# Layer 0: norms, up-projections and rotation in one stage, with split f32r products of 384 columns

## The reference, cut to what matters

```python
p = h @ w_in                                  # 1024 -> 384 + 256 + 32 + 512 + 128 + 128
cq, ckv, kr, gq, gk, gv = split(p)
qa  = rmsnorm(cq, q_norm) @ w_q_up            # 384 -> 8 heads x (64 + 32)
kva = rmsnorm(ckv, kv_norm) @ w_kv_up         # 256 -> 8 heads x (64 keys + 64 values)
# rotation (latent tokens only) of the last 32 of each qa head, of kr, and of the heads of gq and gk
qa = concat([q_nope, rope(q_rope)]) * 96 ** -0.5
ka = concat([k_nope, rope(kr) for every head])
qb, kb = rope(rmsnorm(gq)) * 64 ** -0.5, rope(rmsnorm(gk))
```

## Time and profile before

| what | value |
|---|---|
| median of three runs | 3511.75 us (3507.56 to 3515.62) |
| profiled execution, its own time | 3518.39 us |
| its span in the trace | 3516.5 us |
| granted clock of TensorE, mean | 0.931 |
| busy in the span: TensorE, weight load, VectorE, ScalarE, GpSimd | 88%, 61%, 41%, 22%, 7% |
| input projection of layer 0, to | 157.0 us |
| norms, up-projections, rotations | 157.0 to 299.3 us |
| attention of layer 0 | from 299.3 us |

### The profile page before, as it was taken

One profiled execution on the slowest core, in us unless ns is written; L12 is line 12 of the kernel. 1 busy time (PEld: TensorE's weight loads), 2 busy tenths in 40 slices (PEclk: granted clock), 3 DMA queues, 4 the chain that ended last, 5 costly groups with the idle time before them and its releaser, 6 DMA issues. The chain is left out here.

```text
span 3516.5 us, 48978 instructions
## 1 busy us (share of the span) xinstructions
PE 3104.1 (88%) x19193; PEld 2127.7 (61%) x19193; DVE 1457.6 (41%) x2568; ACT 761.2 (22%) x1482; POOL 237.0 (7%) x435
## 2 busy tenths in 40 slices
PE   7999998799886599977987759989999999899998
PEld 5734667333333598753333337867888788678886
DVE  4316564300000533852000026455555683655555
ACT  3114571211111302821111111142110111221101
POOL 0000040111111200001111110000000000000000
PEclk9999999899998699988998769999999999999998
DMA  7376812999998422349999973113334164123421
GB/s 259 123 269 153 207 18 95 384 419 419 419 419 349 132 72 61 74 164 388 419 419 418 419 283 115 60 49 90 95 107 109 39 104 61 49 72 95 125 72 54
DMA packets 352386, 675.09 MB, mean 192 GB/s; under 512 B 68643, under 2 KB 277636, under 8 KB 296775
## 3 DMA queue, kind: packets, MB, share of 16 engines
q1 hardware_dynamic: 336460, 635.42, 52.0%
q0 software_dynamic: 13664, 31.49, 2.5%
q10 hardware_dynamic: 2067, 5.48, 0.4%
HBM read 642.80 MB, written 45.09 MB: 196 GB/s over the span
## 5 line engine op out<-in xcount | busy, mean ns | idle before, releaser
L3838 ACT ACTIVATE ffn_mixed<-ffn_mixed 128x512 f32<-128x512 f32 x44 | 27.8, 632 | 393.8 <-DVE ffn_mixed L3759 393.8
L2054 DVE TENSOR_TENSOR moe0b_hidden<-moe0b_hidden,moe0b_wide_ps 64x512 f32<-64x512 f32 (+1 forms) x21 | 12.7, 602 | 229.1 <-ACT moe0b_hidden L2051 229.1
L2039 PE MATMUL moe0b_wide_ps<-moe_raw,moe0b_feats 128*64 128x512 f32 x208 | 95.7, 610 | 9.5 <-DMA moe_raw<-in_moe_w_up 9.5
L2054 DVE TENSOR_TENSOR moe1b_hidden<-moe1b_hidden,moe1b_wide_ps 64x512 f32<-64x512 f32 (+1 forms) x18 | 10.3, 573 | 224.1 <-ACT moe1b_hidden L2051 224.1
L2054 DVE TENSOR_TENSOR moe0b_second<-moe0b_second,moe0b_wide_ps 64x512 f32<-64x512 f32 (+1 forms) x20 | 12.2, 611 | 208.1 <-ACT moe0b_second L2051 208.1
L2054 DVE TENSOR_TENSOR moe1b_second<-moe1b_second,moe1b_wide_ps 64x512 f32<-64x512 f32 (+1 forms) x18 | 10.3, 572 | 211.4 <-ACT moe1b_second L2051 211.4
L2040 PE MATMUL moe0b_wide_ps<-moe_raw,moe0b_feats 128*64 128x512 f32 x208 | 95.9, 612 | 0.0
L3756 DVE TENSOR_SCALAR ffn_mixed<-ffn_gate_ps,all_cols 128x512 f32<-128x512 f32 x44 | 35.6, 810 | 145.3 <-PE ffn_up_ps L3688 141.1
L1496 DVE TENSOR_REDUCE attn_top<-attn_scores 128x1 f32<-128x768 f32 (+1 forms) x96 | 72.3, 776 | 37.1 <-PE attn_scores L1409 37.0
L1465 ACT ACTIVATE attn_probs_t<-attn_turned 128x512 f32<-128x512 f32 x112 | 63.4, 604 | 78.9 <-PE attn_turned L1423 78.9
L243 POOL CAST second_first_hi<-all_ahead 128x1024 fp32r<-128x1024 f32 x8 | 9.8, 1223 | 982.6 <-DMA all_ahead<-in_ffn_w_up 696.7
(11 more groups left out here) (998 smaller groups left out, 8681.3 us busy)
## 6 DMA issues: line engine op xcount, KB each, us to landing
moe_raw<-in_moe_w_gate SPq DMA_DIRECT2D x88, 1024.0 KB, 27.3
moe_raw<-in_moe_w_up SPq DMA_DIRECT2D x88, 1024.0 KB, 27.9
moe_raw<-in_moe_w_down SPq DMA_DIRECT2D x86, 1024.0 KB, 28.4
all_ahead<-in_ffn_w_up SPq DMA_DIRECT2D x88, 512.0 KB, 5.1
all_h<-in_moe_w_gate SPq DMA_DIRECT2D x26, 1024.0 KB, 26.8
all_h<-in_w_ada SPq DMA_DIRECT2D x23, 1024.0 KB, 5.5
all_h<-in_moe_w_down SPq DMA_DIRECT2D x21, 1024.0 KB, 28.3
ffn_down<-in_ffn_w_down SPq DMA_DIRECT2D x40, 512.0 KB, 3.6
```

Source lines behind the costliest of these rows:

```text
L2039: nc.tensor.matmul(wide_ps[n][LOW, :], x[:, c, :], gate[:, at], start=c == 0, stop=c == DC - 1)
L2054: return nc.vector.tensor_tensor(hidden[n][HIGH, 0:cols], hidden[n][HIGH, 0:cols], wide_ps[n][HIGH, 0:cols], ALU.mult)
L3838: nc.scalar.activation(mixed[s][:], mixed[s][:], ACT.Silu).then_inc(silu_ready, 1)
```

## The change

The three stages after the input projection become one, `up_stage`. The up-projections become split f32r products in chunks of 128 features and halves of 384 columns: six chunks of queries (two of them hold the rope rows of four heads each, the other four hold two heads each), four of keys, and the values as tiles by tokens. The query chunks are multiplied before the norm is known: the gain is in the rounded input, and the root is multiplied when the result is taken. Two pairs of PSUM banks (`slot`) are used in turn in the order of `UP_USES`; `enter` waits until the pair's former content was taken. The rotations of the eight heads become two turns, so there are 8 turns in place of 14; two key chunks stand ahead of the first. GpSimd takes a share: it splits the query weights in ab_in (`LatentWeights`) and the key and value weights here, squares five chunks, and multiplies by the cosines. VectorE keeps the rest. The query weights are fetched in ab_in, in six transfers with pieces of 32 and 64 values, the key and value weights in four with pieces of 64; the rope tables are fetched after the last query chunk. Units 16 to 23 move into ab_in, whose 13 units now use two slots in `P.h` (one low half of a slab takes the third place); the later 24 units use three slots. Below, VectorE's list is cut where the keys begin, and ScalarE's is left out.

```diff
+                if h == 1 and rotary is not None:
+                    rotary.wait(dve)
                 V.tensor_copy(w_hi[h % 2][:], raw_slab(P, h)).then_inc(w_rounded, 1)
...
-def latent_norm_stage(nc, P, K, tag, parts, eps, ahead, beside):
...
-def product_stage(nc, P, tag, loads, products, engines=("act", "dve"), banks=8, ahead=None, beside=None):
...
-def rope_stage(nc, P, tag, tables, items, spread, beside, distances):
...
+    def start(self, sp):
+        heads = rows_of(self.A["mla_w_q_up"][0]).rearrange("p c (h e) -> p c h e", h=H_A)
+        for c in range(self.QC):
+            sp.dma_start(self.raw[:, c, 0:H_A * ROPE_A].rearrange("p (h e) -> p h e", h=H_A), heads[:, c, :, NOPE_A:]).then_inc(self.landed, 16)
+            sp.dma_start(self.raw[:, c, H_A * ROPE_A:].rearrange("p (h e) -> p h e", h=H_A), heads[:, c, :, 0:NOPE_A]).then_inc(self.landed, 16)
+
+    def pool(self, nc, pool):
+        pool.wait_ge(self.landed, 32 * self.QC)
+        for c in range(self.QC):
+            nc.gpsimd.tensor_copy(self.hi[:, c, :], self.raw[:, c, :]).then_inc(self.rounded, 1)
+            pool.wait_ge(self.rounded, c + 1)
+            nc.gpsimd.tensor_tensor(self.lo[:, c, :], self.raw[:, c, :], self.hi[:, c, :].bitcast(F32), ALU.subtract).then_inc(self.split, 1)
...
+UP_USES = (("q0", 1, 1), ("cq", 2, 1), ("q1", 1, 1), ("q2", 1, 1), ("ckv", 2, 1), ("q3", 1, 1), ("q4", 1, 1), ("q5", 1, 1),
+           ("k0", 1, 2), ("k1", 1, 2), ("turn0", 1, 1), ("k2", 1, 2), ("turn1", 1, 1), ("k3", 1, 2), ("turn2", 1, 1),
+           ("gq0", 2, 1), ("v0", 1, 1), ("gq1", 2, 1), ("turn3", 1, 1), ("v1", 1, 1), ("turn4", 1, 1), ("gq2", 2, 1), ("v2", 1, 1),
+           ("turn5", 1, 1), ("gq3", 2, 1), ("gk", 2, 1), ("turn6", 1, 1), ("turn7", 1, 1), ("distance", 1, 1))
...
+    HALF, RING = TOK // 2, 3
+    slots = Slots(UP_USES)
...
+        free = P.h[:].rearrange("p c n -> p (c n)")[:, ada.GROUP:]
+        cq_hi = over(nc, "up_cq_hi", [PART, QC, TOK], P.h_at + 4 * ada.GROUP)
+        ckv_hi = over(nc, "up_ckv_hi", [PART, KVC, TOK], P.h_at + 4 * ada.GROUP + 4 * QC * TOK)
+        cq_lo, ckv_lo = lows
...
+            heads = rows_of(A["mla_w_kv_up"][0]).rearrange("p c (h e) -> p c h e", h=H_A)
+            for n, part in enumerate((slice(0, NOPE_A), slice(NOPE_A, NOPE_A + V_A))):
+                for c in range(KVC):
+                    at = slice(n * H_A * NOPE_A, (n + 1) * H_A * NOPE_A)
+                    sp.dma_start(wkv[:, c, at].rearrange("p (h e) -> p h e", h=H_A), heads[:, c, :, part]).then_inc(wkv_in, 16)
+            sp.dma_start(swap[:], K["swap_b"]).then_inc(tables_in, 16)
+            sp.dma_start(distances.bias[0:T5_BUCKETS, :], A["rel_bias_2"]).then_inc(distances.ins, 16)
+            sp.dma_start(distances.bias[T5_BUCKETS:, :], K["ones"][0:1, 0:DSA_H]).then_inc(distances.ins, 16)
+            for u in range(27, 33):
+                ada.fetch(sp, u)
...
+            sp.wait_ge(ready, slots.made["q5"])
+            for q in range(QUADS):
+                sp.dma_start(rope_q[q * QUAD:(q + 1) * QUAD], K["rope_a"][rope_rows]).then_inc(tables_in, 16)
+            sp.dma_start(rope_g, K["rope_b"]).then_inc(tables_in, 16)
+            for u in range(33, 43):
+                ada.fetch(sp, u)
+            sp.wait_ge(rotated, 3)
...
+            def q_rows(name, c, j):
+                cols = slice(j * PART, (j + 1) * PART)
+                for k, (w, x) in enumerate(((wq.hi, cq_hi), (wq.hi, cq_lo), (wq.lo, cq_hi))):
+                    for h in range(2):
+                        last = T.matmul(slot[slots.at[name]][:, h, 0:HALF], w[:, c, cols], x[:, c, h * HALF:(h + 1) * HALF],
+                                        start=c == 0 and k == 0, stop=c == QC - 1 and k == 2)
+                return last
+
...
+            ada.multiply(pe, 24)
+            pe.wait_ge(cq_split, 1)
+            q_rows("q0", 0, 0)
+            pe.wait_ge(sums_in, 16)
+            add_square(0)
+            add_square(1)
+            pe.wait_ge(cq_split, 2)
+            q_rows("q0", 1, 0)
+            add_square(2)
+            add_square(3)
+            add_square(4)
+            pe.wait_ge(cq_split, 3)
+            q_rows("q0", 2, 0).then_inc(ready, 1)
+            ada.multiply(pe, 25)
+            ada.multiply(pe, 26)
+            pe.wait_ge(pick_in, 16)
+            spread("cq", NORM_CQ, 0)
+            q_product(1)
+            add_square(FIRST)
+            add_square(FIRST + 1)
+            ada.multiply(pe, 27)
+            q_product(2)
+            add_square(FIRST + 2)
+            add_square(FIRST + 3)
+            spread("ckv", NORM_CKV, 0)
+            add_square(FIRST + 4)
+            ada.multiply(pe, 28)
+            q_product(3)
+            ada.multiply(pe, 29)
+            q_product(4)
+            ada.multiply(pe, 30)
+            q_product(5)
+            ada.multiply(pe, 31)
+
+            pe.wait_ge(wkv_split, 2)
+            pe.wait_ge(ckv_split, KVC)
+            k_product(0)
+            ada.multiply(pe, 32)
+            k_product(1)
+            ada.multiply(pe, 33)
+            ada.turn(pe, 3)
+            pe.wait_ge(tables_in, 16 * (2 + QUADS))
+            turn(0)
+            ada.multiply(pe, 34)
+            k_product(2)
+            ada.multiply(pe, 35)
+            emptied(pe, "q0")
+            turn(1)
+            ada.multiply(pe, 36)
+            k_product(3)
+            ada.multiply(pe, 37)
+            emptied(pe, "q1")
+            turn(2)
+            spread("gq0", 0, 1)
+            ada.multiply(pe, 38)
+            v_product(0)
+            ada.multiply(pe, 39)
+            spread("gq1", 1, 1)
+            ada.multiply(pe, 40)
+            emptied(pe, "gq0")
...
+            emptied(pe, "gq3")
+            turn(6)
+            ada.turn(pe, 5)
+            emptied(pe, "gk")
+            turn(7)
+            pe.wait_ge(distances.ins, 48)
+            enter("distance")
+            for h, (a, e) in enumerate(((0, BANK), (BANK, distances.SPAN))):
+                last = T.matmul(wide_rows("distance")[0:DSA_H, h, 0:e - a], distances.bias[:], distances.by_bucket[:, a:e], start=True, stop=True)
+            last.then_inc(ready, 1)
...
+            def low_q(c):
+                V.scalar_tensor_tensor(cq_lo[:, c, :], cq[:, c, :], gain("mla_q_norm", c), cq_hi[:, c, :].bitcast(F32), ALU.mult, ALU.subtract).then_inc(cq_split, 1)
...
+            V.tensor_tensor(squares[0], cq[:, 0, :], cq[:, 0, :], ALU.mult).then_inc(squared_by["dve"], 1)
+            dve.wait_ge(squared_by["dve"], 1)
+            dve.wait_ge(cq_rounded, 1)
+            low_q(0)
+            dve.wait_ge(squared_by["pool"], 1)
+            dve.wait_ge(cq_rounded, 2)
+            low_q(1)
+            dve.wait_ge(squared_by["act"], 1)
+            dve.wait_ge(cq_rounded, 3)
+            low_q(2)
+            dve.wait_ge(rooted, 1)
+            V.reciprocal(root[:, 0, :], root[:, 0, :]).then_inc(inverted, 1)
+            emptied(dve, "cq")
+            take_rope(0)
+            take_rope(1)
+            take_heads(0)
+            dve.wait_ge(squared_by["pool"], 2)
+            dve.wait_ge(squared_by["act"], 2)
+            scale("ckv", ckv[:, 0, :], gain("mla_kv_norm", 0)).then_inc(ckv_scaled, 1)
+            release(scale("ckv", ckv[:, 1, :], gain("mla_kv_norm", 1)), "ckv")
+            take_heads(1)
+            for c in range(KVC):
+                dve.wait_ge(ckv_rounded, c + 1)
+                low(ckv_lo[:, c, :], ckv[:, c, :], ckv_hi[:, c, :]).then_inc(ckv_split, 1)
+            take_heads(2)
+            dve.wait_ge(rooted, 2)
+            V.reciprocal(root[:, 1, :], root[:, 1, :]).then_inc(inverted, 1)
+            take_heads(3)
+
...
+            square(1, cq[:, 1, :])
+            square(4, ckv[:, 1, :])
+            for c in range(3):
+                square(5 + c, gq[:, c, :])
+            for n in range(2):
+                part = slice(n * H_A * NOPE_A, (n + 1) * H_A * NOPE_A)
+                pool.wait_ge(wkv_rounded, n + 1)
+                G_.tensor_tensor(wkv_lo[:, :, part], wkv[:, :, part], wkv_hi[:, :, part].bitcast(F32), ALU.subtract).then_inc(wkv_split, 1)
+            pool.wait_ge(ready, slots.made["q5"])
+            pool.wait_ge(tables_in, 16 * (2 + QUADS))
+            pool.wait_ge(wkv_split, 2)
+            cosine(0)
+            pool.wait_ge(cos_done, 1)
+            for f in range(2):
+                emptied(pool, f"q{f}")
+                cosine(1 + f)
+            for c in range(G):
+                emptied(pool, f"gq{c}")
+                cosine(3 + c)
+            emptied(pool, "gk")
+            cosine(3 + G)
...
-            own = [sb(f"ada_slot{n}", [PART, ada.GROUP])[:] for n in range(2)]
...
-            units = range(FIRST_UNITS, 2 * DC)
-            ada.place("in", own + [P.h[:].rearrange("p c n -> p (c n)")[:, n * ada.GROUP:(n + 1) * ada.GROUP] for n in range(3)], units)
-            early, late = units[0:2], units[2:]
-
+            units = range(FIRST_UNITS, 3 * DC)
+            ada.place("in", ada_slots[0:2], units)
```

(22 more changed lines are left out.)

## The result

The median goes from 3511.11 us (3507.56 to 3515.62, four runs) to 3472.44 us (3467.61 to 3477.47, four runs): a ratio of 0.9889, with an interval of 0.9871 to 0.9908, so 32 to 45 us less. Predicted were 3472 us and 40 us less. In two further sets of runs on other chips the kernel before had medians of 3517.84 and 3514.09 us, and the changed kernel, in the second, 3473.16 us (ratio 0.9882, 0.9863 to 0.9901).

The account below looks back on a forecast made before the run. TensorE was fullest throughout, partly waiting with VectorE. Work 84.6 plus waits 5.2 gave 89.8 us for 142.3, 52.5 less; minus 12.1 and 0.5 in the input projection, about 40 less: 3472 us, range 3459 to 3486.

Parts of the forecast that it names:

- The sum of TensorE's work and of the changes between f32 and f32r: New stage: TensorE's work 81.2 us plus 3.4 for 17 islands of f32 work between f32r products, 84.6 us.
- The low bound of 0.120 us: New stage: a 384-column f32r product might cost as little as a 256-column one, 0.120 us; 0.174 was taken.
- rival 4: Up-projections: 384-column f32r products cost what f32 ones do, 0.67 us, making the kernel 37 us slower; chance 0.01.
- Wait (a): Stage opening: first f32r product waits for ScalarE's rounding and VectorE's square and subtraction, with GpSimd squaring at once; 2.8 us.
- Wait (b): Second query chunk waits until VectorE empties its pair of banks, after the spread root has been copied; 1.9 us.
- Wait (c): New stage: unit 33 stands behind the five rope-table transfers on SP's queue and comes about 0.5 us late.
- Later units come in time: Units after 33 don't wait: each slot is asked for some 9 us earlier, and 1 MB lands in 5.5 us.
- rival 3: New stage: transfers of units bind; slow turns make it 5 us longer; chance 0.08 for a few us, 0.03 for slower kernel.
- the likeliest case: Whole kernel: 36 to 44 us gained, around 3472 us; chance 0.51.
- rivals 1 and 2: Rival 1: in the rotations the VectorE-GpSimd lock becomes the bound, costing 4 to 10 us; chance 0.15. Rival 2: own line.
- rival 2: Clock: low in the stage's opening costs 3 to 5 us, or full in attention's opening returns 4.3; chance 0.2 together.
- All later stages shifted, not changed: Sign expected in the changed kernel's profile: stages after the new one start earlier but keep their lengths.

Follow-up runs that it names:

- root_earlier: Changed kernel with the query root's spread product ahead of unit 26 instead of behind it: stage 92.6 us, whole 3480.3 us (one run).
- changed with 24 waits: Changed kernel with TensorE's wait ahead of the distance product issued 24 times instead of once: stage 96.8 us, whole 3481.5 us (one run).

## Why the prediction was right

**The new stage, 93.1 us where 89.8 were expected.** The sum of TensorE's work and of the changes between f32 and f32r held: 84.4 us measured against 84.6, and so did its terms one by one: a chunk of 18 query products took 3.36 us with the change to f32 behind it (181.62 to 184.98), where 3.13 + 0.2 was in the sum. The low bound of 0.120 us for a product of 384 columns, and with it rival 4, fell (0.177).

**Wait (a), the opening, expected 2.8, measured 1.2.** The first low part was ready 1.94 us after the unit began (168.97 to 170.91), where 2.0 was the figure without a quarrel. The step that failed is that GpSimd squares at the same time: its first square began at 170.22, when VectorE's square (168.81, 0.96 us) was done and its first low part was on its way. GpSimd's and VectorE's timelines show that the quarrel came behind that:

```profile
170.22 1.96 POOL L1550 TENSOR_TENSOR l_va<-l_cq 128x768 f32<-128x768 f32 x1 [95.11 <-issue]
```

```profile
169.84 1.02 DVE L1376 SCALAR_TENSOR_TENSOR l_cq_lo<-l_cq,all_cols,up_cq_hi 128x768 fp32r<-128x768 f32 x1
172.22 3.19 DVE L1376 SCALAR_TENSOR_TENSOR l_cq_lo<-l_cq,all_cols,up_cq_hi 128x768 fp32r<-128x768 f32 x2 [1.36 <-POOL l_va L1550]
```

VectorE waited 1.36 us until GpSimd's square was done; that is a wait of the program (`squared_by["pool"]`), and no lock. But this square had taken 1.96 us where a later one took 1.47, and VectorE's two following parts took 3.19 where two of 1.02 are 2.04, while GpSimd squared again from 173.13 to 174.60. TensorE saw only 0.28 us of it, since sums of squares stood between. By the rule of the Trainium skill (SBUF — State Buffer, Who interferes with whom) these pairs shut each other out; the lengthened durations agree with it.

**Wait (b), 1.9 us, measured 1.94**, and root_earlier takes 1.0 of it away.

**Wait (c), unit 33, expected 0.5, measured 1.32.** The unit landed 5.7 us after it was asked for (207.36 to 213.04), as quickly as expected; it was asked for late. SP's timeline:

```profile
205.13 1.72 SPq L1216 DMA_DIRECT2D l_cq<-const_rope_a  x4
206.89 0.42 SPq L1217 DMA_DIRECT2D l_cq<-const_rope_b  x1
207.36 0.90 SPq L416 DMA_DIRECT2D all_ahead<-in_w_ada  x2
...
242.48 2.18 SPq L416 DMA_DIRECT2D all_ahead<-in_w_ada  x2
```

Its slot was free at 201.7, when unit 30 was multiplied, but SP waited for the last query chunk (205.1), and then issuing the five tables took it 2.2 us, which the sum leaves out.

**The term that was mis-sized: "Later units come in time".** Both of its figures were wrong. Landing was taken at 5.5 us from the earlier trace rows, a median over 250 us. Transfers of the changed stage, and below them those of the kernel before from 265.5 to 299.3 us, its rotations; count, KB each, median us to landing:

```profile
all_ahead<-in_w_ada SPq DMA_DIRECT2D x14, 1024.0 KB, 7.1
all_h<-in_w_ada SPq DMA_DIRECT2D x7, 1024.0 KB, 7.6
```

```profile
all_h<-in_w_ada SPq DMA_DIRECT2D x4, 1024.0 KB, 7.9
all_ahead<-in_w_ada SPq DMA_DIRECT2D x2, 1024.0 KB, 8.9
```

So the trace of the kernel before had the higher figure, where units stood close as they do in the new rotations; in its up-projections the medians are 4.9 and 5.0. In the changed stage it is the same: with three slots throughout, the median is 4.9 for the three units asked for between 186 and 198 us, each when the one before had landed, and 8.2 for the seven asked for from 228.8 us on, where two or three are under way. And the time between asking and use was not 9 us: 7.1, 6.7 and 6.8 us for units 38, 41 and 45, which landed after 7.5, 7.1 and 8.5 and so waited 0.4, 0.4 and 1.8.

The waits for units are 3.9 to 4.3 us, and the run without transfers is 4.5 to 4.9 shorter; the prediction had 0.5, and its rival 3 "a few us" for 5 more. The size is that of the mild form of rival 3, within the likeliest case, but not its way: a turn of 7.3 + 1.2 us, eight times, is 68 us and far below the stage's 93, so the slots bind in places, and not all through. The run with two slots shows the same mechanism at 15.8 us. A fourth slot wasn't tried.

The key and value weights were taken at 4.6 us from transfers that are alike in size only the earlier trace rows: their four strided transfers landed in 6.1 us and took SP 5.7 us to issue. Nothing waited for it.

**The rivals 1 and 2.** The lock didn't bind: the rotations' additions took 0.69 us each, as before, since each cosine had ended before its addition, as the prediction says against this rival, and the cosines could be moved away for nothing. The clock in attention's opening was 0.53 (before 0.60), 0.50 to 0.60 in all other profiles but two, so nothing was lost or won there: that TensorE's denser stage should lift it was wrong. The two exceptions are the stages without transfers (0.69) and with two slots (1.00). The low clock in the new stage's opening, which rival 2 put at 3 to 5 us, wasn't there in the profiled execution; in four other profiles it was (0.79 over the first 8 us) and cost some 1.2 us.

**The input projection, expected 12.1 us more.** From its first to its last product it took 102.4 and 102.6 us before and 114.5 in the profiled execution, so 12.0 more; the ten profiles of changed kernels lie between 113.7 and 116.0. The pairs of units waited 1.0, 0.8 and 0.7 us, 2.6 in place of 1.9:

```profile
123.61 1.06 PE L425 MATMUL ada_acc<-all_h,all_cond 128*32 128x512 f32 x8 [1.01 <-DMA all_h<-in_w_ada]
```

```profile
137.00 1.06 PE L425 MATMUL ada_acc<-all_h,all_cond 128*32 128x512 f32 x8 [0.83 <-DMA all_h<-in_w_ada]
```

The split of the query weights on GpSimd ran into VectorE's slab and cost TensorE nothing that shows: the slab was split at 68.03 us, as before (last section).

**"All later stages shifted, not changed"** was wrong by the experts' step. By the profiled executions 45.8 us were won: 37.2 up to attention, 5.4 at that step (21.8 to 16.5), and 3.2 of what differs from run to run. By repeated profiles the stage and the input projection give 49 - 12 = 37, and the step 5: 42, beside 38.7 and 40.9 us between medians. So that the number came out to within 1 to 2 us is luck in part. Two misses nearly cancelled: the stage is 3.3 us longer than forecast, since 3.4 us of waits for units and 1.7 of low clock were missing from the sum, against 1.6 too much for the opening, and some 5 us were won by where TensorE's instructions stand, which no part of the change was meant to do. Without them the 37 us would still lie within the forecast of 36 to 44.

## What to carry to other kernels

When a stage is made denser, the landing time of its transfers must be read where they are asked for as closely as they will be then, and not as a median over a longer time: here 5.5 us stood for 5 and 8 to 9. It is to be set against the time between asking and use of each unit, read from the order of the queue. Waits for units were 3.9 of the 7.0 us of waits in the new stage. Cheaper products were the smallest part of this gain (4 of 49 us); larger chunks, fewer turns, fewer units and one block in place of three made the rest, by an estimate from the cadences, so price such an edit part by part. Profile the changed kernel more than twice before a few us of a stage are put down to anything. And a difference in a stage that the change doesn't touch can be due to where the instructions stand: shift the stream of the kernel before with waits that cost little before it is put down to the change.

## What the runs showed of the hardware

**The place in TensorE's stream.** 23 and 59 further instructions, all of them waits long fulfilled, took 4.5 and 5.6 us of idle time away some 860 us later (one profile each), where TensorE skips the bodies of four tests. The mechanism isn't shown. The Trainium skill (Runtime: NRT & Kernel Launch, Instruction fetch mechanics) says that instructions come in blocks of 16 KB through a DMA queue of their own, and that a taken branch to a place outside the blocks at hand waits for a fetch. The traces have such transfers of about 16 KB. The last one ahead of this step lies 21 to 22 us before it in the two profiles with the loss and 16 to 19 us in seven without, in all but one of the nine within about 1 us of the start of the idle time. That fits the rule, but it doesn't show that the fetch is what is waited for.

**VectorE and GpSimd in the input projection**, on unlike operations. Their timelines, first GpSimd's:

```profile
61.71 4.17 POOL L1097 CAST l_wq_hi<-l_ka 128x768 fp32r<-128x768 f32 x1 [61.28 <-DMA l_ka<-in_mla_w_q_up]
65.96 3.78 POOL L1099 TENSOR_TENSOR l_wq_lo<-l_ka,l_wq_hi 128x768 fp32r<-128x768 f32 x1
69.68 0.82 POOL L1097 CAST l_wq_hi<-l_ka 128x768 fp32r<-128x768 f32 x1
70.58 1.84 POOL L1099 TENSOR_TENSOR l_wq_lo<-l_ka,l_wq_hi 128x768 fp32r<-128x768 f32 x1
```

```profile
65.23 2.80 DVE L935 TENSOR_TENSOR ab_in_last_low<-all_ahead,ab_in_w_hi 128x2048 fp32r<-128x2048 f32 x1
...
73.89 2.30 DVE L933 CAST ab_in_w_hi<-all_ahead 128x2048 fp32r<-128x2048 f32 x1
```

GpSimd's cast took 4.17 us beside VectorE's dense splitting and 0.82 beside its idleness; its subtraction 3.78 and 1.84. VectorE's 2048-column subtraction took 2.80 where 2.29 is usual, and its cast 2.30, where the one at 63.98 in the same trace took 1.22, while GpSimd subtracted from 73.27 on. So either engine can be the one that is held up, and a cast with one input too.

**The clock in the stage.** Nearly the same instructions met a low clock at different places. In the first profile of the changed kernel it was 0.57 for 4 us behind unit 45's wait of 1.8 us, with 1.00 before, and the first key product started 37.1 us after the stage. In its second profile and with the cosines on VectorE it was 0.79 from about 12 to 20 us, and the key product started at 38.6. In three others (no transfers, one key chunk ahead, changed with 24 waits) it was 0.79 in the first 8 us, and the key product started at 38.2 to 38.4. With f32 products it was 1.00 throughout. So such a stretch costs this stage 1.2 to 1.7 us; why it comes where it does isn't settled.

**The clock at attention's opening** was at 0.50 to 0.60 in twelve of fourteen profiles, and at 1.00 in the one whose stage had nine waits for transfers, up to 4.5 us. More idle time of TensorE before it did not lower it there. Why isn't settled.
